# Local attention three tiles deep, and latent queries evicted by two engines, in a decoder kernel

## What is computed

```python
def _mla_attend(q_nope, q_rope, k_nope, k_rope, v):        # 8 heads, causal over 512 keys
    s = (q_nope . k_nope + q_rope . k_rope) * 96 ** -0.5
    w = softmax(where(causal, s, NEG_INF));  return w @ v
def _swa_attend(q, k, v, sinks, rel_bias):                 # 8 heads, 2 kv heads, window 128
    s = q . k * 64 ** -0.5 + bias                          # keys of own and previous 128-block
    w = softmax(concatenate([s, sink]))[..., :-1];  return w @ v
```

## Time and profile before

| | |
|---|---|
| runs of the kernel | median 2626.5 us (3 runs, 2622.18 to 2627.39) |
| the profiled execution's own time | 2628.38 us, its span 2626.5 us |
| PE busy | 2529.6 us (96%) |
| DVE / ACT / POOL busy | 1319.1 / 919.7 / 1161.7 us |
| granted PE clock, mean | 0.987 of full speed |
| DMA | 203.19 MB, mean 77 GB/s |
| latent attention with its input, both groups | about 83 to 174 us |
| local attention | about 185 to 240 us |

### The profile page before, as it was taken

One profiled execution on the slowest core, in us unless ns is written; L12 is line 12 of the kernel. 1 busy time (PEld: TensorE's weight loads), 2 busy tenths in 40 slices (PEclk: granted clock), 3 DMA queues, 4 the chain that ended last, 5 costly groups with the idle time before them and its releaser, 6 DMA issues.

```text
span 2626.5 us, 47068 instructions
## 1 busy us (share of the span) xinstructions
PE 2529.6 (96%) x18452; PEld 2067.2 (79%) x18452; DVE 1319.1 (50%) x1976; ACT 919.7 (35%) x1471; POOL 1161.7 (44%) x688
## 2 busy tenths in 40 slices
PE   8888899999999998999999999999999999999997
PEld 6666688887786876888877888888888878788886
DVE  3655873354504158633456755556658883321113
ACT  4333422222634234222235433333345553332221
POOL 4433544444544445444445322323347754444442
PEclk9999999999999999999999999999999999999999
DMA  6210233323220212323322111111113323232331
GB/s 175 83 41 25 80 96 96 96 96 96 80 96 25 81 33 88 96 96 96 97 88 86 50 43 35 36 49 40 37 50 98 96 80 104 88 99 93 96 97 55
DMA packets 57721, 203.19 MB, mean 77 GB/s; under 512 B 6449, under 2 KB 9177, under 8 KB 57561
## 3 DMA queue, kind: packets, MB, share of 16 engines
q1 hardware_dynamic: 54288, 196.37, 23.4%
q10 hardware_dynamic: 2920, 3.44, 0.7%
q0 software_dynamic: 352, 1.05, 0.1%
HBM read 197.17 MB, written 3.67 MB: 76 GB/s over the span
## 4 chain that ended last, share of the span: by engine, by line
PE 88%; DVE 6%; ACT 3%; issue 1%; POOL 1%; DMA 0%; SPq 0%; DVEq 0%; ACTq 0%; POOLq 0%
PE banks L1908 24%; PE banks L1910 24%; PE banks L1909 24%; PE banks L2350 9%; ACT sb_pa L621 1%; PE banks L2400 1%; PE banks L2118 1%; POOL sb_pa L1795 1%; DVE sb_x L1130 1%; PE banks L2101 1%; PE banks L2041 1%; PE banks L2080 1%; PE banks L2260 1%; PE banks L2251 1%; DVE sb_w L1127 1%
## 5 line engine op out<-in xcount | busy, mean ns | idle before, releaser
L1769 POOL TENSOR_TENSOR sb_wl<-sb_raw,sb_wh 128x1024 fp32r<-128x1024 f32 (+1 forms) x366 | 884.2, 2419 | 1051.9 <-ACT sb_wh L464 1051.4
L1908 PE MATMUL banks<-sb_bh,sb_wh 128*128 128x512 f32 x2656 | 1055.3, 397 | 46.3 <-POOL sb_bl L1781 23.9
L1909 PE MATMUL banks<-sb_bl,sb_wh 128*128 128x512 f32 x2656 | 1042.8, 393 | 0.0
L1910 PE MATMUL banks<-sb_bh,sb_wl 128*128 128x512 f32 x2656 | 1042.8, 393 | 0.0
L1908 PEld LDWEIGHTS banks<-sb_bh,sb_wh 128*128 128x128 f32 x2656 | 502.7, 189 | 172.2 <-issue 47.6
L1910 PEld LDWEIGHTS banks<-sb_bh,sb_wl 128*128 128x128 f32 x2656 | 502.4, 189 | 109.4
L1909 PEld LDWEIGHTS banks<-sb_bl,sb_wh 128*128 128x128 f32 x2656 | 503.1, 189 | 107.0 <-issue 2.2
L464 ACT CAST sb_wh<-sb_raw 128x1024 fp32r<-128x1024 f32 (+1 forms) x366 | 376.5, 1031 | 484.9 <-PE banks L1910 481.8
L2350 PEld LDWEIGHTS banks<-sb_m 64*64 64x64 f32 x5632 | 195.9, 134 | 16.7 <-issue 8.0
L1050 DVE SCALAR_TENSOR_TENSOR sb_x<-sb_x,banks 128x512 f32 x72 | 49.5, 688 | 315.0 <-PE banks L1910 315.0
L2350 PE MATMUL banks<-sb_m 64*64 64x64 f32 (+1 forms) x5632 | 206.8, 229 | 0.6 <-DVE sb_m L1604 0.2
(11 more groups left out here) (343 smaller groups left out, 2640.1 us busy)
## 6 DMA issues: line engine op xcount, KB each, us to landing
sb_raw<-w SPq DMA_DIRECT2D x366, 512.0 KB, 3.5
sb_x<-xT SPq DMA_DIRECT2D x4, 512.0 KB, 7.0
out<-sb_x SPq DMA_DIRECT2D x4, 512.0 KB, 2.6
bias_rows<-sb_brow ACTq DMA_DIRECT2D x1, 1536.0 KB
sb_pj<-pT POOLq DMA_DIRECT2D x2, 512.0 KB, 4.0
sb_t<-bias_rows ACTq DMA_DIRECT2D x1, 512.0 KB, 3.7
sb_sq<-bias_rows ACTq DMA_DIRECT2D x1, 512.0 KB, 4.7
sb_wm<-wm ACTq DMA_DIRECT2D x1, 288.0 KB, 2.9
```

Source lines behind the costliest of these rows:

```text
L1769: nc.gpsimd.tensor_tensor(wl[:, s, 0:cols], raw[:, s, 0:cols], wh[:, s, 0:cols].bitcast(F32), ALU.subtract).then_inc(lo_ready, 1)
L1908: nc.tensor.matmul(out, hi_a, hi_b, start=first, stop=False)
L1909: nc.tensor.matmul(out, hi_a, lo_b, start=False, stop=False)
L1910: return nc.tensor.matmul(out, lo_a, hi_b, start=False, stop=last)
```

## The change

**Local attention.** The lead of `scores`, `maxima` and `exps` over `turn` is three tiles instead of two. Scores use five banks (3 to 7) in turn, one per tile and head, so that two and a half tiles fit. The transposes of both heads of a tile lie side by side in bank 2, and DVE copies them with one instruction, after both are there. DVE also waits for its own last maximum before it overwrites `snk`. RING stays 3. The latent attention and the attention of the second block keep their lead and banks.

**Query tiles of `mla_in`.** ACT makes the scaled copy of the plain features, between its roundings of panels; DVE only rotates, and waits for ACT's copy (`qa_copied`) ahead of the last instruction, so that the bank is still given back once.

```diff
+        def ahead(kind):
+            return 3 if kind == "swa" else 2
+
+        def score_bank(kind, t, e):
+
+            return 3 + (2 * t + e) % 5 if kind == "swa" else 4 + 2 * (t % 2) + e
...
# ACT
-                steps(NB * units, ((2, exps), (-2, high)))
+                steps(NB * units, ((ahead(kind), exps), (-2, high)))
...
             def mla_in(grp):
 
-                for i in range(4):
-                    split(Idx(0, w.p + 3 + i))
+                if grp:
+                    act.wait_ge(s_ready, 2 * w.t)
+                split(Idx(0, w.p + 3))
+                split(Idx(0, w.p + 4))
+                for t in range(4):
+                    if t % 2 == 0:
+                        act.wait_ge(mid_done, w.mid + 2 + t // 2)
+                    else:
+                        act.wait_ge(panel_done, w.p + 2 + t // 2)
+                    nc.scalar.activation(qa[0:64, t, :], psum[0:64, (w.g + 2 + t) % 2, :], ACT.Copy,
+                                         scale=MLA_SCALE).then_inc(qa_copied, 1)
+                    if t % 2:
+                        split(Idx(0, w.p + 5 + t // 2))
...
# DVE
+                    if kind == "swa" and j:
+                        dve.wait_ge(nm_ready, 2 * t)
...
+                    if kind == "swa":
+                        dve.wait_ge(pt_ready, 2 * t + 2)
+                        turned_pair = w4.rearrange("p (a e n) -> p a e n", a=2, e=2)[:, t % 2, :, 0:width]
+                        nc.vector.tensor_copy(turned_pair, psum[:, 2, :].rearrange("p (e n) -> p e n", e=2)[:, :, 0:width]
+                                              ).then_inc(pt_copied, 2)
+                        return
...
-                steps(NB * units, ((1, inverses), (2, maxima), (0, turned), (-2, low)))
+                steps(NB * units, ((1, inverses), (ahead(kind), maxima), (0, turned), (-2, low)))
...
+                if copied:
+                    dve.wait_ge(qa_copied, copied)
                 for d in dst:
                     last = nc.vector.tensor_tensor(d, rt[64:96, 0, :], rt[64:96, 1, :], ALU.add)
...
-                    nc.vector.tensor_scalar(qa[0:64, t, :], psum[0:64, b, :], MLA_SCALE, None, ALU.mult)
-                    rotate([qa[64:96, t, :]], b, MLA_SCALE).then_inc(bank_free[b], 1)
+                    rotate([qa[64:96, t, :]], b, MLA_SCALE, 4 * grp + t + 1).then_inc(bank_free[b], 1)
...
# PE
-                        if t >= 2:
+                        if kind == "swa":
+                            pe.wait_ge(exp_done, max(2 * t + e - 4, 2 * t0))
+                            if j == 0:
+                                pe.wait_ge(pt_copied, 2 * t0)
+                        elif t >= 2:
                             pe.wait_ge(exp_done, 2 * (t - 2) + e + 1)
...
                         if t >= 1:
-                            pe.wait_ge(pt_copied, 2 * (t - 1) + e + 1)
+                            pe.wait_ge(pt_copied, 2 * t if kind == "swa" else 2 * (t - 1) + e + 1)
                         for c in range(0, width, P):
-                            last = nc.tensor.transpose(psum[:, 2 + e, c:c + P], pa[:, t % RING, e, c:c + P], ident[:, :])
+                            out = psum[:, 2, 2 * P * e + c:2 * P * e + c + P] if kind == "swa" else psum[:, 2 + e, c:c + P]
+                            last = nc.tensor.transpose(out, pa[:, t % RING, e, c:c + P], ident[:, :])
...
-                steps(NB * units, ((2, scores), (0, turn), (-1, values)))
+                steps(NB * units, ((ahead(kind), scores), (0, turn), (-1, values)))
```

More of the change, by code:

```diff
@@ L297, in build @@
         tap_ready, tap_used = sem("tap_ready"), sem("tap_used")
+        qa_copied = sem("qa_copied")
         y_total, y_low = sem("y_total"), sem("y_low")
@@ L620, in exps @@
                         act.wait_ge(nm_ready, 2 * t + e + 1)
-                        nc.scalar.activation(pa[:, ring, e, 0:width], psum[:, 4 + 2 * (t % 2) + e, 0:width], ACT.Exp,
+                        nc.scalar.activation(pa[:, ring, e, 0:width], psum[:, score_bank(kind, t, e), 0:width], ACT.Exp,
                                              bias=nm[:, ring, e:e + 1], accum_out=sm[:, ring, e:e + 1]).then_inc(exp_done, 1)
@@ L1248, in maxima @@
                     width, _ = span(kind, i)
+                    if kind == "swa" and j:
+                        dve.wait_ge(nm_ready, 2 * t)
                     for e in range(2):
                         dve.wait_ge(s_ready, 2 * t + e + 1)
-                        s_i = psum[:, 4 + 2 * (t % 2) + e, 0:width]
+                        s_i = psum[:, score_bank(kind, t, e), 0:width]
                         if kind == "swa":
@@ L1285, in low, with rotate @@
                                                 ALU.subtract).then_inc(bank_free[b], 1)
-                steps(NB * units, ((1, inverses), (2, maxima), (0, turned), (-2, low)))
+                steps(NB * units, ((1, inverses), (ahead(kind), maxima), (0, turned), (-2, low)))
                 w.t += NB * units
                 w.g += units
-            def rotate(dst, b, scale):
+            def rotate(dst, b, scale, copied=0):
                 nc.vector.scalar_tensor_tensor(rt[64:96, 0, :], psum[96:128, b, :], scale, rope[96:128, :], ALU.mult, ALU.mult)
@@ L2068, in scores @@
                     width, kb = span(kind, i)
-                    out = [psum[:, 4 + 2 * (t % 2) + e, 0:width] for e in range(2)]
+                    out = [psum[:, score_bank(kind, t, e), 0:width] for e in range(2)]
                     rows = [slice(64 * e, 64 * e + 64) for e in range(2)]
```

## The result

| | before | changed |
|---|---|---|
| median, us | 2624.97 (5 runs, 2622.18 to 2627.39) | 2610.41 (5 runs, 2608.08 to 2611.69) |
| ratio, 95% interval | | 0.994 (0.993 to 0.9951) |
| the profiled execution's own time, its span | 2628.38, 2626.5 | 2608.08, 2606.2 |
| PE / DVE / ACT / POOL busy | 2529.6 / 1319.1 / 919.7 / 1161.7 | 2520.6 / 1314.6 / 923.9 / 1159.6 |

14.6 us less, against 14.7 forecast; the interval allows 12.9 to 18.4. The two profiled executions differ by 20.3 us, since that of the kernel before (2628.38) lies above its five runs and that of the changed kernel is the fastest of its five; the medians tell the size, the traces the place.

A forecast was written before the change was run, and what follows sets the result against it. TensorE carries 88% of the waits, but a serial loop of VectorE and ScalarE held the local attention. Gains of 12.0 there and 2.7 on query tiles, 14.7 us, take 2628.38 to 2613.7, median about 2612; range 2605 to 2619.

The forecast's parts named there:

- The loop and its bound: Local attention: lead three cuts the VectorE-ScalarE loop, TensorE bounds; wide tile 3.22 to 2.72 us, stage 55.4 to 43.4.
- The two additions: Local attention, on top of 39.6 us: 2.3 idle from the last tile's 6.9 us latency, and 1.5 at the subtractions.
- The three subtractions: Local attention: VectorE's high-part subtraction waits for ScalarE once per head pair; 0.5 us lost on TensorE each, bounds 0 and 1.6.
- The edits put at nothing: Local attention: five score banks, one transpose bank with one copy, RING at 3 and VectorE's wait on its last maximum cost 0.
- a new wait of PE for the merged copy: Local attention: a sign that the prediction is wrong, TensorE newly waiting for VectorE's single copy of both heads' transposes; no size given.
- The query tiles: Ahead of each latent attention: moving the copy gains 1.35 us a group, 2.7 in all, not 2.8 a group.
- two adds still longer: Query tiles: a sign expected in the profile after, two of VectorE's last adds still taking over 0.68 us.
- All later stages have the same lengths: Rest of the kernel: a sign expected in the profile after, no later stage moves.
- DVE as bound: Local attention rival, 12%: VectorE becomes the bound, wide tiles 3.0 us, stage 50.3, total 2618 to 2619.
- The lead without effect: Local attention rival, 6%: with RING 3 the lead doesn't help, 3.22 us stays, only 2.7 gained, total 2624.
- Exclusion on a bank: Query tiles rival, 5%: ScalarE and VectorE exclude each other on a bank, the tiles gain nothing, total 2614.7.
- A falling clock in the local attention: Local attention rival, 3%: TensorE's granted clock falls to 1.2 GHz, slower, 2652 us if all its work is hit.

The follow-up runs named there:

- high part first: Changed kernel with ScalarE's high part of a finished head pair ahead of the step's exponentials in the local attention; 2610.48 us, ratio 0.9941 to the kernel before.
- six places: Changed kernel with six places instead of three for probabilities, maxima, sums and inverses in the local attention; 2610.67 us, ratio 0.9935 to the kernel before.
- changed again: The changed kernel run once more with nothing altered; 2610.39 us, ratio 0.9944 to the kernel before.
- query part only: Kernel before with only the query tiles' scaled copy moved to ScalarE, local attention as before; 2623.94 us, ratio 0.999 to the kernel before.

## Why the prediction was right

**The loop and its bound.** Right in mechanism and size. The wide tile came to 2.72 and 2.71 us (2.72 forecast), the stage to 43.3 (43.4), the wait of the exponentials went down, DVE waits for PE's scores. They did not stop waiting, as the prediction has it among its signs; 1.3 to 1.4 us a wide tile is left. Putting the lead back alone brought 3.22 and 55.25 back.

**The two additions.** The latency at the end was 7.05 us (6.9 forecast). The three subtractions were put at 1.5 us; the high part first gave back 1.07. The term was a little large. The 4.6 us of PE work behind the last scores are called older work in the prediction; they hold the last tile's own transposes and values (3.5 us are older), and with these the sum is right.

**The edits put at nothing.** The ring of three cost nothing and the merged copy is worth 0.3 us. The five score banks and the one bank of transposes changed nothing with the lead at two; at three they can't be taken away, so there only the total speaks for them. The prediction named a new wait of PE for the merged copy as a sign of being wrong. There is such a wait, 1.7 us in four, but it is what is left of 8.6 us in eight. Two of the four stand at the subtractions (0.34 each) and two at the end of the stage.

**The query tiles.** The forecast that 5.6 at face value would come to 2.7, because POOL's subtraction stands in the way, holds: 1.56 or 1.40 a group on the two branches (1.35 forecast), 3.0 to 3.1 together in the three traces where the clock held, 1.9 to 2.1 in the three where it fell once; 2.5 in the median of that part alone. Both outcomes of the race were worked out from durations of before. The "two adds still longer" came only with DVE first; with POOL first there is one.

**What the sum left out.** The stage's end at full clock gave 1.2 us more, named only as an end of the range. And PE's longer single stop in the query tiles sometimes costs clock: in three of the twelve groups, all with the single long sum, tile 3 came late (tiles of 12.0 to 12.2 us in the table). These are of opposite sign. Windows of the two traces give 12.1 for the local attention, 2.75 for the two latent groups (3.1 on the tiles, the rest the clock and scatter) and 1.2 behind the stage, 16.1 in all where the medians give 14.6. So the mechanism and its two terms hold, but that the total was met within 0.1 is luck: the interval is 12.9 to 18.4. "All later stages have the same lengths" holds but for that 1.2 and for the scatter of the rest.

**The rivals.** DVE as bound: no, it waits for scores. The lead without effect: no, and six places changed nothing. Exclusion on a bank: no, by the joint reads and by the kernel that forbids them. A falling clock in the local attention: 1.00 throughout, where the window before had 0.96 in all, for its last 3.3 us at 0.50.

## What to carry to other kernels

Where two in-order engines wait for each other in turn, look at which stage stands ahead of which in a step. One more tile of lead cuts the loop, and the period becomes the busiest engine's work between starts; extra buffers are only its price. Before moving work off an engine, find which of its instructions share a port with another engine and when that one comes: here GpSimd's subtraction took about half of what the moved copy was worth, and putting it off (its result is read only after the attention) brought 4.4 us on the tiles, where the moved copies had brought 3.1 at most.

## What the runs showed of the hardware that was not expected

The race between VectorE and GpSimd falls either way from one group to the next, with recorded starts within 10 ns of each other, and these don't tell who wins. POOL was first with 90.22 against DVE's 90.23 (changed) and with 89.16 on both (six places); DVE was first with 90.07 on both (changed again) and even with POOL recorded at 136.06 and DVE at 136.07 (high part first, group 1). The loser waits for nearly all of the winner's instruction: 2.90 for a sum of 0.68 behind a subtraction of 2.36, or 2.96 for that subtraction behind the sum.

The granted clock fell behind a stop of TensorE of 2 us in some groups and not in others. The third query product waits for the long sum, 2.05 us in group 0 of the first changed trace and 2.01 in group 1 of the second. In the first the clock stayed at 1.00 behind it; in the second it did not:

```profile
134.00:138.00 4.00, 2.95 (x12) 1.80 (x10) 3.81 (x5) 2.12 (x3) 1.73 (x1) 1.00 0.47 143
138.00:142.00 4.00, 2.78 (x9) 2.21 (x10) 3.24 (x4) 0.00 (x0) 0.63 (x1) 0.79 0.43 131
```

Full clock from 134 to 138, 0.79 in the mean of the next 4 us, and there tile 3 ended 1 us late (tiles 12.09 in place of 11.12). The same happened in group 0 of the query part only (a stop of 2.06, then 0.64 over 4 us) and of the six places (2.01, then 0.66). The ends of the latent attentions, tabled above, are alike: the same gaps, and 1.00 in twelve of the 26 ends on record. Why one group meets it and a like one doesn't was not settled.
